# New order tables for VectorE, ScalarE and the page fetches of a decoder layer

## The reference, cut to what matters

```python
z = rmsnorm(x) @ w_in                                    # 2048 -> 3920 columns
mla = attention(q(z), k(z), v(z))                        # sample tokens also read 2048 cached positions through a page table
gla = gated_linear_attention(z)                          # chunks, a carried state
h = x + concat(rmsnorm(mla), gla) @ w_out
q = (rmsnorm(h) @ peer_w_q).reshape(t, 8, 2, 128)        # PEER: 8 heads, two key halves
v1, i1 = top_k(q[:, :, 0] @ keys1.T, 16); v2, i2 = top_k(q[:, :, 1] @ keys2.T, 16)
top_s, e = top_k(v1[..., None] + v2[..., None, :], 16)   # 16 experts of 16384 per token and head
act = gelu(einsum("td,thkd->thk", xn, peer_u[e]))        # 128 rows of peer_u per token
h = h + einsum("thk,thkd->td", softmax(top_s) * act, peer_v[e])
y = h + sigmoid(rmsnorm(h) @ w_ple_gate) * (p @ w_ple_proj)
```

## Time and profile before

| | before |
|---|---|
| time, median of 3 runs | 4336.06 us (4333.66 to 4340.84) |
| span of the profiled execution | 4331.6 us, 4.5 us under that median |
| PE busy | 2254.9 us (52%) |
| DVE busy | 3288.1 us (76%) |
| ACT busy | 522.0 us (12%) |
| POOL busy | 2201.2 us (51%) |
| moved by DMA | 1599.51 MB, mean 369 GB/s |
| q0 (POOL's gathers) / q1 (SP, ACT) | 72.0% / 19.5% of 16 engines' span |
| L1993, rows of peer_v | 571 instructions, mean 2350 ns, 188.0 us idle before |
| L1968, rows of peer_u | 576 instructions, mean 2287 ns, 169.4 us idle before |
| L1373, norm steps on DVE | 20 instructions, 225.8 us idle before |

### The profile page before, as it was taken

The page is one execution under the profiler, slowest core; times in us unless marked ns, Lnnn a source line. Parts: engine busy times, 40 slices in busy tenths (PEclk is TensorE's granted clock), DMA queues, the critical chain, the costliest instruction groups (busy, mean ns, idle before and its releaser), DMA issues.

```text
span 4331.6 us, 24058 instructions
## 1 busy us (share of the span) xinstructions
PE 2254.9 (52%) x8238; PEld 1342.1 (31%) x8238; DVE 3288.1 (76%) x3700; ACT 522.0 (12%) x1098; POOL 2201.2 (51%) x1216
## 2 busy tenths in 40 slices
PE   8999815425899492779942457710000920000755
PEld 4456403213475131367731222710000410000322
DVE  0130699997667998868889856699999699988673
ACT  2220112122002001212212010000001000001001
POOL 0000365744332556468775653345667368877441
PEclk9999956657999796767865678955555965555877
DMA  8658789988997999989999899988989999999996
GB/s 294 250 223 287 303 357 364 422 323 335 424 423 299 422 424 414 353 356 365 406 374 360 347 400 413 405 345 339 399 365 405 424 415 422 422 407 422 424 408 234
DMA packets 261153, 1599.51 MB, mean 369 GB/s; under 512 B 27763, under 2 KB 49459, under 8 KB 91750
## 3 DMA queue, kind: packets, MB, share of 16 engines
q0 software_dynamic: 176064, 1268.30, 72.0%
q1 hardware_dynamic: 83078, 320.64, 19.5%
q10 hardware_dynamic: 1888, 9.03, 0.5%
HBM read 1554.75 MB, written 42.56 MB: 369 GB/s over the span
## 4 chain that ended last, share of the span: by engine, by line
PE 31%; DVE 30%; POOL 16%; DMA 13%; issue 7%; ACT 2%; SPq 0%; DVEq 0%; ACTq 0%; POOLq 0%
POOL ring L2549 16%; PE bank L826 14%; DVE ring L1968 11%; DVE total L1993 9%; DMA ring<-in_peer_v,idx_all 5%; DMA ring<-in_peer_u,idx_all 5%; PE bank L1251 4%; PE bank L1288 3%; PE bank L929 1%; PE bank L891 1%; PE bank L800 1%; PE bank L1079 1%; DMA front<-in_cache_kv_latent,page_rows 1%; DVE front L1744 1%; PE bank L1093 1%
## 5 line engine op out<-in xcount | busy, mean ns | idle before, releaser
L1993 DVE SCALAR_TENSOR_TENSOR total<-ring,gate_all,total 128x2048 f32<-128x2048 f32 x571 | 1341.8, 2350 | 188.0 <-DMA ring<-in_peer_v,idx_all 164.5
L2549 POOL DMA_INDIRECT ring<-in_peer_u,idx_all x576 | 1062.2, 1844 | 795.7 <-DVE total L1993 359.1
L2549 POOL DMA_INDIRECT ring<-in_peer_v,idx_all x576 | 1072.2, 1861 | 711.9 <-DVE total L1993 376.3
L1968 DVE CUSTOM_DVE_ANT_0 ring<-ring,xrow 128x2048 f32<-128x2048 f32 x576 | 1297.5, 2287 | 169.4 <-DMA ring<-in_peer_u,idx_all 167.5
L826 PE MATMUL bank<-front 128*128 128x512 f32 (+3 forms) x1920 | 838.3, 594 | 68.9 <-ACT front L2115 64.6
L800 PE MATMUL bank<-inv_diag,front 128*128 128x128 f32 (+1 forms) x304 | 61.9, 391 | 1159.3 <-DVE inv_diag L1378 1102.2
L826 PEld LDWEIGHTS bank<-front 128*128 128x128 f32 (+1 forms) x1920 | 338.4, 181 | 558.5 <-issue 554.5
L800 PEld LDWEIGHTS bank<-inv_diag,front 128*128 128x128 f32 (+1 forms) x304 | 58.9, 299 | 1164.2 <-DVE inv_diag L1378 1098.2
L1251 PE MATMUL bank<-front 128*128 128x128 f32 (+2 forms) x1536 | 257.0, 329 | 20.5 <-DMA front<-in_peer_w_q 17.4
L1251 PEld LDWEIGHTS bank<-front 128*128 128x128 f32 x1536 | 239.8, 192 | 39.3 <-DMA front<-in_peer_w_q 20.3
L2574 POOL DMA_DIRECT2D ring<-in_w_in x12 | 10.7, 894 | 342.8 <-PE bank L1288 239.6
(11 more groups left out here) (323 smaller groups left out, 2894.0 us busy)
## 6 DMA issues: line engine op xcount, KB each, us to landing
front<-in_w_in SPq DMA_DIRECT2D x64, 980.0 KB, 8.4
front<-in_w_out SPq DMA_DIRECT2D x48, 1024.0 KB, 9.1
front<-in_peer_w_q SPq DMA_DIRECT2D x48, 1024.0 KB, 13.3
front<-in_w_ple_gate SPq DMA_DIRECT2D x48, 1024.0 KB, 9.1
ring<-in_w_in POOLq DMA_DIRECT2D x12, 1960.0 KB, 10.5
front<-in_w_uq SPq DMA_DIRECT2D x6, 1536.0 KB, 10.7
ring<-in_peer_u,idx_all POOLq DMA_INDIRECT x576, 14.3
ring<-in_peer_v,idx_all POOLq DMA_INDIRECT x576, 16.0
```

The costliest lines, as they stand in the source:

```text
L1968: e.tensor_tensor_reduce(out=ring[:, b, :], in0=ring[:, b, :], in1=xrow[:, t % 2, :], scale=1.0, scalar=0.0, op0=ALU.mult, op1=ALU.add, ac ...
L1993: e.scalar_tensor_tensor(out=total, in0=ring[:, b, :], scalar=c1, in1=total, op0=ALU.mult, op1=ALU.add).then_inc(s("summed"), 1)
L2549: e.indirect_dma_start(out=ring[:, k % RING, :], out_offset=None, in_=a[("peer_u", "peer_v")[side]][0], in_offset=bass.IndirectOffsetOnAxi ...
```

## The change

Three tables get other values. Each has as many as before: 16, 705 and 36. No instruction is added, taken away or altered; the order of instructions changes on DVE (steps against rows), on ACT (Gelus against steps) and on POOL (page fetches against gathers).

```diff
-PAGES_BEFORE = [395, 395, 395, 402, 404, 414, 414, 426, 428, 440, 440, 451, 452, 462, 467, 476]
+PAGES_BEFORE = [
+    377, 385, 385, 389, 406, 410, 410, 424, 424, 436, 436, 452, 460, 465, 465, 481]
 ROWS_BEFORE = [
-    0, 0, 0, 0, 0, 0, 0, 0, 0, 0, 0, 0, 0, 0, 0, 0, 0, 0, 0, 0, 0, 0, 5, 5, 5, 16, 17, 18, 18, 18, 18, 18, 18, 18, 18,
...
+    0, 0, 0, 0, 3, 3, 3, 3, 3, 4, 4, 4, 4, 7, 7, 7, 7, 8, 9, 10, 10, 11, 12, 12, 12, 12, 14, 14, 15, 15, 21, 21,
...
 STEPS_BEFORE = [
-    0, 10, 39, 66, 81, 97, 111, 119, 138, 139, 146, 175, 212, 244, 244, 274, 278, 296, 299, 320, 327, 327, 327, 330, 330,
-    330, 333, 345, 345, 345, 345, 345, 345, 348, 381, 394]
+    0, 1, 51, 55, 94, 114, 115, 135, 139, 144, 167, 181, 215, 218, 244, 264, 276, 291, 308, 321, 322, 326, 327,
+    327, 328, 329, 329, 329, 329, 330, 330, 331, 345, 348, 518, 586]
```

## The result

The changed kernel takes 4376.53 us (median of 4 runs, 4372.93 to 4380.41) beside 4338.45 us for the kernel before on the same chip: ratio 1.0087, 95% interval 1.0072 to 1.0101, so 38 us slower (31 to 44). The forecast was 4352 us with a range of 4302 to 4395: right in sign and inside the range, 24 us short. Of the change itself it had less than half: 16.4 us on the span, which grew from 4331.6 to 4371.1 us, by 39.5 us. The wide range held faster, same and slower alike, and slower had a chance of 0.50. Every line number of VectorE's code is 4 higher than before.

The account below looks back on a forecast made before the run. Most stages were taken as bound by DVE, three by PE's chain, and from 3325.1 us on by transfers. Stage terms summed to +16.4 us on a span of 4331.6, plus 4.5 to the median: 4352 us, range 4302 to 4395.

Parts of the forecast that it names:

- the three waits: Start to step 211: with fewer rows ahead, waits at steps 87, 107 and 211 grow by 13, 14 and 14.6 us.
- Stages 220 to 323 and 561 to 675: First: 45 rows become 36, -30.2 us; second: 167 rows become 335, +392.8 us.
- the tail: After the last row: step 704 goes from row 1124 to 1144, fewer rows hide its path, +11 us (0 to +20).
- Unit 34's Gelu: Waits for embedding(1)'s sigmoids, some 18 us late near row 1121; DVE makes most of it good, +2 us.
- rival (b): Slower: trips keep 28 to 32 us (+13), unit 34's Gelu not made good (+18 to 22); about 4387 us, chance 0.18.
- Rival (a), short trips: Faster: round trips short once DVE pauses, three waits cost nothing (-41.6), state chain -6; 4304 us, chance 0.27.
- a gain of 5 us: Start to step 211: other idle time may shrink by 5 us, as the top-k steps are spread.
- 10 us to the load behind step 345: Stage 343 to 396: steps 345 to 348 need a load, one row there instead of 14, some 10 us of idle.
- The 16 us I had counted back: Stage 343 to 396: 12 more rows late in the stage fill most of its 27.0 us of idle, -16 us.
- Thirteen rows are had for nothing: Sample attention, steps 396 to 452: 101 rows become 114, yet the stage takes 330 us, -2.6 us.
- That is the chain's length: Stage 536 to 552: 49.1 us from last state update to step 552 stays as long; stage +6 us (0 to +14).
- 159 rows at 2.49 us: Step 675 to the last row, DMA-bound: 321 rows become 162, -395.9 us; whole stage -393.9 us.

Follow-up runs that it names:

- new_quiet_store: The changed kernel with steps 100 to 105 moved to row 108, where step 106 stands: 4383.71 us (1.0103).
- new_gap_107: The changed kernel with steps 107 to 213 eleven rows later each: 4396.63 us (1.0141).
- new_old_early: The changed kernel with steps 0 to 44 at the old rows and the second Gelu behind ten steps as before: 4355.16 us (1.0038).
- new_gap_348: The changed kernel with 14 rows between steps 345 and 348 instead of one, steps behind following more closely until 379: 4364.24 us (1.0053).
- new_even_attention: The changed kernel with steps 396 to 451 over the same 114 rows in the old table's pattern, page fetches and Gelus 13 to 15 moved along: 4368.21 us (1.0055).
- old_half_late: Old tables to step 560, new from 561, but steps 561 to 682 midway between old and new rows (new values under 664 raised to 664): 4327.55 us (0.9967).

## Why the forecast was right, and where it was not

**Right: the sign, two of the three waits, and most stages.** Steps 107 and 211 waited 16.2 and 18.3 us; I had 14 at 107 and 22 at 211 in all. Stages 220 to 323 and 561 to 675 and the tail came within 6 us. Unit 34's Gelu ran at 4191.75 us, 4 us before row 1121 (4195.84), where I had it late; so rival (b) had no ground. Rival (a), short trips, was true at steps 87 and 552 and false at 107 and 211; at 107 the queue decided, by new_quiet_store.

**Not shown: that these waits made the kernel slower.** new_quiet_store and new_gap_107 both took away the wait before step 107, and neither was faster (4383.71 and 4396.63 us beside 4376.53). The three changes that did gain time mend losses that the forecast did not have, or had at half their size: new_old_early 21 us, new_gap_348 12 to 15, new_even_attention 8 to 14. Whether they add up was not run.

**Luck.** The norms' idle time rose by 43.8 us where I said 40, but not where I said: I had 22 us before step 211 and 45 before step 552, and they waited 18.3 and 12.8. The rise came at step 215 (8.4 to 23.3 us) and at the four norms of the first two embeddings (7.7 to 35.3 in all). The total is near for the same reason: the misses below are 14, 22, 55, -29 and -17 us. The sign rests on a sum of +16 us whose largest miss was 55.

**Wrong, and cancelling in part.**
1. Start to step 211, 14 us too low. "Three waits grow": I looked only at steps whose gap to their predecessor had shrunk. The 14.5 us at step 50 come from a step that moved back (42, row 18 to 33) and holds a buffer that a load needs. The 13.8 us at step 28 come from the top-k steps that were spread between rows; I had counted that as a gain of 5 us. new_old_early shows that the early part of the tables makes both. Against them stands the wait at 87 that did not come.
2. Stage 343 to 396, 22 us too low. I gave 10 us to the load behind step 345; DVE waited 21.4 for it. The 16 us I had counted back did not come, since step 396 waited 13.2 us for PE.
3. Stage 396 to 452, 55 us too low, the largest miss. "Thirteen rows are had for nothing": I bounded it by DVE's and DMA's sums, and neither was the bound. PE was busy 303.89 of 332.6 us: it was the bound, through steps that alternate with DVE. With 13 rows more among them and another order PE's waits grew, the granted clock of the stage fell from 0.77 to 0.69, and its 1732 matmuls took 328.71 us. new_even_attention gave 22.7 us of the 52.7 back by the order alone.
4. Stage 536 to 552, 29 us too high. "That is the chain's length" took a trip of 27.3 us for fixed; it was 3.3.
5. From step 675 on 17 us too high: 159 rows at 2.49 us were taken out; they took 411.0 us with them, 2.58 each. The earlier trace rows are a calm stretch; the stage as a whole moved 413 GB/s, which makes 2.54 of a row of 1.05 MB. In old_half_late 80 rows were worth 2.50 each. The other 79 of the 159 rows were worth 2.63 each (933.8 less 726.0 us), but there the embeddings move too. So a part of the 17 us is not the price of a row, and what it is stays open.

The sum of all misses, the small ones too, is +23 us.

## What to carry to other kernels

Price a store's or load's round trip by what is queued at its issue, packet against packet, not by its bytes; steps placed together just ahead of it, or work held back just behind it, took it here from 25 us to 4 and from 27 to 3. Count what the steps cost: in new_quiet_store it was as much as the wait had. When rows of a shared engine are moved between stages, ask of each stage for the step on which the slow engine's chain hangs: rows up to it were free here (141.2 to 141.7 us with 25 or 36 rows), and in the chain that alternates with DVE 13 rows cost their full 30 us. When a table is redone as a whole, cut old against new where both stand at the same count, and keep the better half: here that gave 4318.24 us where the new table had lost 38 us, and a cut further on, at step 561, gave 4307.74.

## What the hardware showed that I had not expected

Two queues shared the engines by packets, not bytes: 1376 packets of 1.1 KB took turns with 1427 of 7.3 KB and got 14.5% of the engines. The same work on PE (1732 or 1733 matmuls in sample attention) took 303.89 us at a mean granted clock of 0.77, 318.91 at 0.71 and 328.71 at 0.69, while PE stood still for 28.7, 43.7 and 56.6 us: the stage with more time lost between the instructions had the lower clock and the longer instructions. With the old table this stage took 330.4 to 351.2 us in six profiles of different kernels, with the new one 382.2 to 389.2 in six; whether that spread is also what sets two runs of one kernel apart was not tried.
